# Hybrid mLSTM, stick-breaking and PEER layer: head scores through a per-tile query in place of folded query weights

## The chip, the cores and the metric

One core of a Trainium2 chip runs the whole layer. The metric is the device time of one execution in microseconds; the median of three is given for the kernel before. Engines: PE is TensorE, DVE is VectorE, ACT is ScalarE, POOL is GpSimd, SP is SyncE.

## What is computed

The input has 1024 tokens of width 1024 behind a lead tile that holds 16 meta tokens, so there are nine tiles of 128 tokens. A layer normalises, projects, runs two mixers (an mLSTM with 4 heads and a stick-breaking attention with 8 heads), adds the result to the residual, and then runs a PEER feed-forward: each token has 8 heads, each head picks 16 of 16384 experts. The change touches how a head is scored and one product of the attention:

```python
# peer_ffn, one tile of 128 tokens
q = (xt @ w_query).reshape(T, Hh, 2, PEER_HALF)
s = jnp.einsum('thpc,pnc->thpn', q, sub_keys)
sv, si = lax.top_k(s, K)
...
act = jax.nn.gelu(jnp.einsum('td,thkd->thk', xt, expert_u[eidx]))
return jnp.einsum('thk,thkd->td', g * act, expert_v[eidx])
# stick_breaking_mixer, a block of 128 queries
z = jnp.einsum('bhtd,bhsd->bhts', qb, kh)     # 8 heads of width 64
```

## The kernel before

**Three stages.** In the front PE projects the tiles (a "unit" is one tile and one of six sections of the input weights, written to the tile `xs`) and mixes tile 1. Then comes a stream of slots, numbered from -16. In slot s POOL gathers one row of `expert_u` and one of `expert_v` for each of 128 tokens (512 KB each, an indirect DMA), DVE multiplies the `expert_u` row with the token's row and sums it (L2021, "dot"), and every fourth slot PE adds four `expert_v` rows into `acc` (`sum_set`). Sixteen slots are a head, 128 a tile. Rows wait in rings of slots: four for U and six for V at first, more later (`U_RINGS`, `V_RINGS`). Six tiles go through the stream (`PASSES`); tiles 4 and 6 are "dense": from slot 564 (`DENSE_AT`) on all 16384 experts are computed for them in 128 blocks over 200 slots, on PE (`dense_z`, `dense_out`), while the last gathers run beside it.

**What sets the order.** Every engine has one program, written out slot by slot, and runs it strictly in its order with semaphore waits. The loops at the end of `scalar`, `vector` and `tensor` blocks say what an engine does in a slot. Mixing tile M (2 to 8) is spread over slots from `MIX_AT[M]` on (36, 112, 176, 240, 304, 368, 434); `mixed_at(s)` gives the piece of a slot. Key block i of tile M is one attention step: `z` on PE, three ACT operations for each half of the heads (`ln_z`), DVE `make_sp`, `s` on PE, `exp_a` on ACT, `av` on PE. `hg` is the half: heads of even and odd number, which lie in partitions 0 to 63 and 64 to 127, and whose results go to two different PSUM banks. There are 44 such steps, each with eight `z` products.

**Scoring.** 64 heads are scored (8 tiles of 8 heads, `ROUTED`), head R in slot `SCORES_AT[R]`: heads 0 to 2 in the front's list `ITEMS`, heads 3 to 7 in slots 20, 36, 52, 68 and 84, heads 8 to 55 in slots 109 to 490, heads 56 to 63 in slots 564 to 618. Before any of that the query weights are folded with the keys: 32 folds, each four products of `w_queryT` with `subT` into a PSUM bank and one ACT copy of the bank back over the weights (`fold`). 12 folds stand in `ITEMS`, 12 in slots -6 to 11, 8 in slots 53 to 70 (`FOLD_SLOTS`); the first 24 go to `acc`, the rest to the banks of the units. `scores(R)` is then eight products of `n2T` with the folded weights into bank 7. DVE takes the best 16 of each half of the keys (`best_halves`, L1901, four slots after `scores`) and the picks that follow, in seven pieces in slots +4 to +10. Bank 7 is shared with `turn_idx` and `turn_weights`; each use first waits for all readers of it (`bank7_free`).

Within a slot PE does: `sum_set`, `turn_idx`, `turn_weights`, `scores`, a quarter of a unit (`project`), a fold, the mixing piece, then dense work.

## Time and profile before

| | before |
|---|---|
| median of 3 runs | 3098.28 us (3096.65 to 3100.13) |
| profiled execution, its own time | 3102.96 us |
| its span, first to last instruction | 3101.4 us |
| PE busy | 2620.7 us (85%) |
| DVE busy | 2137.8 us (69%) |
| POOL busy | 1621.3 us (52%) |
| ACT busy | 802.4 us (26%) |
| moved by DMA | 1071.75 MB, mean 346 GB/s |
| mean granted TensorE clock | 0.905 |

An f32 matmul of the program stands in the trace as two matmul records, so eight products are x16. A mean duration of a matmul contains the pipeline's latency; how many microseconds a row of matmuls takes from PE is read from the start of one group to the start of the next, or from the chain of waits. Clock 1.00 is 2.4 GHz, and 0.50 is 1.2 GHz.

### The profile page before, as it was taken

How to read it: one execution, taken by the hardware profiler on the slowest of the kernel's cores; microseconds unless marked ns; L12 is line 12 of the kernel's file. 1: busy time of each engine (PE TensorE's matmuls, PEld its weight loads, DVE VectorE, ACT ScalarE, POOL GpSimd, SP SyncE). 2: the span in 40 equal slices, each digit the busy share in tenths (PEclk: the TensorE clock that was granted, in tenths of full speed). 3: DMA queues.
4: the chain of work that ended last, by engine and by line, in shares of the span. 5: the costliest groups of instructions: out<-in, count | busy, mean ns of one | idle time of the engine just before them, and what ended most of it. 6: DMA issues, size and time to landing. Idle time of an engine off the chain costs nothing.

```text
span 3101.4 us, 36389 instructions
## 1 busy us (share of the span) xinstructions
PE 2620.7 (85%) x12372; PEld 1662.7 (54%) x12372; DVE 2137.8 (69%) x5237; ACT 802.4 (26%) x1766; POOL 1621.3 (52%) x1567
## 2 busy tenths in 40 slices
PE   8999998866877767778687787667999999999998
PEld 6898744323444344444354443445666666666664
DVE  5451646457989879887988887774677755565556
ACT  2231213212323223232243243783111101000001
POOL 0000356577666666655656567665445554455544
PEclk9999999977887878988798798778999999999999
DMA  7103689799999999998989999999999999999998
GB/s 260 49 29 140 229 317 345 282 409 364 382 408 370 397 379 381 385 360 322 403 336 386 353 376 388 393 361 403 371 372 378 383 402 402 403 401 401 402 399 303
DMA packets 338896, 1071.75 MB, mean 346 GB/s; under 512 B 33876, under 2 KB 74136, under 8 KB 337688
## 3 DMA queue, kind: packets, MB, share of 16 engines
q0 software_dynamic: 221184, 805.40, 67.3%
q1 hardware_dynamic: 117528, 264.01, 22.8%
q8 instruction: 100, 1.64, 0.2%
q14 instruction: 84, 0.69, 0.1%
HBM read 1029.03 MB, written 40.26 MB: 345 GB/s over the span
## 4 chain that ended last, share of the span: by engine, by line
PE 55%; DVE 17%; DMA 12%; issue 5%; POOL 5%; ACT 4%; SPq 1%; DVEq 0%; ACTq 0%; POOLq 0%
PE bank L2209 20%; PE xs L2209 15%; PE xs_ahead L2209 14%; DVE work L2021 6%; PE acc L2209 6%; DMA weights<-u_blocks 4%; DMA work<-expert_u,chosen 4%; POOL work L1276 3%; POOL work L1256 3%; DMA work<-expert_v,idx_v 2%; DVE work L1673 2%; DVE work L1681 2%; ACT work L1296 1%; DVE rest L1905 1%; DMA out<-y 1%
## 5 line engine op out<-in xcount | busy, mean ns | idle before, releaser
L1256 POOL DMA_INDIRECT work<-expert_u,chosen x716 | 771.9, 1078 | 837.1 <-DVE dots L2021 351.8
L1276 POOL DMA_INDIRECT work<-expert_v,idx_v x516 | 518.6, 1005 | 399.8 <-PE acc L2209 260.3
L2021 DVE CUSTOM_DVE_ANT_0 work<-work,xs 128x1024 f32<-128x1024 f32 x418 | 506.4, 1216 | 62.4 <-DMA work<-expert_u,chosen 51.4
L2209 PE MATMUL xs_ahead<-work 64*128 64x128 f32 (+3 forms) x1746 | 426.1, 402 | 91.1 <-ACT weights L1296 41.2
L2209 PE MATMUL bank<-weights 128*128 128x256 f32 x2016 | 465.8, 385 | 22.8 <-DMA weights<-u_blocks 22.8
L2021 DVE CUSTOM_DVE_ANT_0 work<-work 128x1024 f32<-128x1024 f32 x298 | 364.1, 1223 | 162.2 <-DMA work<-expert_u,chosen 159.1
L2209 PEld LDWEIGHTS bank<-weights 128*128 128x128 f32 x2016 | 388.6, 193 | 130.6 <-issue 54.4
L2209 PE MATMUL acc<-work,lw 128*32 128x512 f32 x2064 | 338.7, 716 | 91.7 <-DMA work<-expert_v,idx_v 89.4
L2209 PEld LDWEIGHTS xs_ahead<-work 128*128 128x128 f32 (+1 forms) x1746 | 261.9, 214 | 245.2 <-issue 199.4
L1673 DVE TENSOR_TENSOR work<-work,weights 128x256 f32<-128x256 f32 x128 | 54.5, 426 | 371.3 <-ACT work L1544 294.7
L2209 PE MATMUL bank<-weights,n2T 128*128 128x256 f32 x1024 | 265.5, 418 | 23.6 <-ACT lw L1296 22.1
L1544 ACT ACTIVATE work<-bank 128x256 f32<-128x256 f32 x128 | 49.2, 384 | 856.5 <-PE bank L2209 856.5
L2209 PEld LDWEIGHTS bank<-weights,n2T 128*128 128x128 f32 x1024 | 215.0, 214 | 83.9 <-issue 51.0
L2209 PE MATMUL xs<-work 128*128 128x512 f32 x512 | 240.6, 592 | 0.0
L2209 PEld LDWEIGHTS acc<-work,lw 128*32 128x32 f32 x2064 | 67.8, 123 | 251.0 <-issue 150.9
L2209 PE MATMUL xs_ahead<-work,neg_tri 128*128 128x512 f32 (+1 forms) x176 | 115.6, 743 | 86.4 <-DVE work L1681 66.0
L2209 PE MATMUL xs<-work,weights 128*128 128x128 f32 x1472 | 173.9, 280 | 3.4 <-DMA weights<-w_in 3.4
L2209 PEld LDWEIGHTS xs<-work,weights 128*128 128x128 f32 x1472 | 170.6, 196 | 6.0 <-DMA weights<-w_in 3.7
L2209 PE MATMUL xs<-weights,work 128*128 128x512 f32 x368 | 170.7, 608 | 0.0
L1673 DVE TENSOR_TENSOR work<-work 128x512 f32<-128x512 f32 (+3 forms) x156 | 127.9, 822 | 61.9 <-PE xs_ahead L2209 43.6
L1276 POOL DMA_INDIRECT work<-expert_v,chosen x112 | 113.2, 1010 | 55.2 <-issue 33.5
L2209 PEld LDWEIGHTS xs<-work 128*128 128x128 f32 x512 | 97.3, 190 | 68.7 <-issue 62.2
(281 smaller groups left out, 3516.2 us busy)
## 6 DMA issues: line engine op xcount, KB each, us to landing
work<-expert_v SPq DMA_DIRECT2D x128, 512.0 KB, 13.7
weights<-u_blocks SPq DMA_DIRECT2D x126, 512.0 KB, 14.6
work<-kv_dram SPq DMA_DIRECT2D x72, 256.0 KB, 6.2
weights<-w_dram SPq DMA_DIRECT2D x32, 512.0 KB, 20.2
w_dram<-weights SPq DMA_DIRECT2D x7, 2048.0 KB, 11.0
weights<-w_in SPq DMA_DIRECT2D x6, 2048.0 KB, 19.3
work<-expert_u,chosen POOLq DMA_INDIRECT x716, 8.6
mix_dram<-work SPq DMA_DIRECT2D x34, 256.0 KB, 3.3
```

Source lines behind the costliest of these rows:

```text
L1256: pool.indirect_dma_start(out=slot(s), out_offset=None, in_=expert_u, in_offset=bass.IndirectOffsetOnAxis(ap=chosen[:, G % PICKED_HEADS, k ...
L1276: pool.indirect_dma_start(out=slot(s), out_offset=None, in_=expert_v, in_offset=bass.IndirectOffsetOnAxis(ap=picks, axis=0)).then_inc(v_la ...
L1296: return nc.scalar.activation(out_, in_, ACT.Copy, scale=scale)
L1544: nc.scalar.activation(g_d[j % D_G], bank[6][:, 0:D_TOKENS], ACT.Gelu).then_inc(gelu_d_ready, 1)
L1673: return nc.vector.tensor_tensor(out_, a, b, op)
L1681: return nc.vector.scalar_tensor_tensor(out=out_, in0=a, scalar=s, in1=b, op0=op0, op1=op1)
L1905: last = nc.vector.match_replace(spare, values[:, 0:8], src, LOWEST)
L2021: nc.vector.tensor_tensor_reduce(slot(s), slot(s), rows, 1.0, 0.0, ALU.mult, ALU.add, dots[:, d:d + 1]).then_inc(dotted, 1)
L2209: return nc.tensor.matmul(out_, lhsT, rhs, start=start, stop=stop, skip_group_check=True)
```

## The change

The folds are gone. For head R, `query(R)` forms the head's query of this tile, transposed: 2 x 8 products of 128 columns, from the unfolded weights and `n2T`, into bank 7. ACT copies it to a new tile `q_T` (`copy_query`), as the first of the scoring-related work of its next slot, and `scores(R)` is two products of 128 columns of `q_T` with `subT`. In PE's slot the query stands where the scores stood, ahead of the mixing piece; the scores come one slot later (`SCORED_AT = 1`), behind the mixing piece of that slot. The weights are loaded from `w_query` in place of its transpose: the same four loads of 2 MB, in rows of 2 KB where there were rows of 4 KB.

The eight `z` products alternate between the halves of the partitions, where four of the one half came before four of the other.

Smaller parts: the tile `before` is dropped and its two uses are made from `neg_tri` (one product more, once); `gate_inv` becomes `gate_sum` in place; ACT's `square_y` and `rs_y` stand ahead in their slots, and write their unused squares over `q_T`, not `subT`.

```diff
-ACC_FOLDS = 24
+SCORED_AT = 1
...
-put(58.3, ("fold", (0, 4)))
+put(58.3, ("query", 0))
 put(59.5, ("scores", 0))
-put(61.5, ("fold", (4, 8)))
+put(62.2, ("query", 1))
 put(62.5, ("soft", 0))
 put(63.5, ("scores", 1))
 put(65.4, ("picks", 0))
-put(65.5, ("fold", (8, 12)))
+put(65.5, ("query", 2))
 put(66.5, ("scores", 2))
...
-                sp.dma_start(w_qT[i], w_queryT.rearrange("(j c) k -> c j k", c=P)[:, i * Q_EACH:(i + 1) * Q_EACH, :]).then_inc(
+                n = Q_EACH * P
+                sp.dma_start(w_q[i], w_query.rearrange("(k p) n -> p k n", p=P)[:, :, i * n:(i + 1) * n]).then_inc(
...
+            def copy_query(G):
+
+                act.wait_ge(query_done, G + 1)
+                wait(act, scores_done, G)
+                copy(q_T[:, :, :], bank[7][:, 0:2 * P].rearrange("p (j t) -> p j t", j=2)).then_inc(query_copied, 1)
...
                     if s % SLOTS == 0 and 2 <= s // SLOTS + 1 < GT:
                         move_rows(s // SLOTS + 1)
-                    if s - 1 in FOLD_SLOTS:
-                        fold(FOLD_SLOTS[s - 1], FOLD_SLOTS[s - 1] + 1)
+                    for f in finishing(T, n - 1):
+                        square_y(f)
+                    for f in finishing(T, n - 3):
+                        rs_y(f)
+                    for R in [R for R in routed_at(s, SCORED_AT) if R > 2]:
+                        copy_query(R)
...
-                for hg in range(2):
-                    r = slice(SD * hg, SD * hg + SD)
-                    for cc in range(SHP):
-
+                for cc in range(SHP):
+                    for hg in range(2):
+                        r = slice(SD * hg, SD * hg + SD)
                         last = mm(bank[4 + hg][0:m, cc * P:(cc + 1) * P], keys_of(T, i)[r, cc, :], qsT[r, cc, :], cc == 0,
                                   False)
-                    last.then_inc(z_done, 1)
+                        if cc == SHP - 1:
+                            last.then_inc(z_done, 1)
...
+            def query(G):
...
+                bank7_free()
+                seven["queries"] += 1
+                for j in range(2):
+                    n = (2 * h % Q_EACH + j) * P
+                    for k in range(KC):
+                        last = mm(bank[7][:, j * P:(j + 1) * P], w_q[2 * h // Q_EACH][:, k, n:n + P], n2T[:, k, :],
+                                  k == 0, k == KC - 1)
+                last.then_inc(query_done, 1)
+
             def scores(G):
...
-                for k in range(KC):
-                    last = mm(bank[7][:, 0:2 * NKEY].rearrange("p (j n) -> p j n", j=2), n2T[:, k, :],
-                              w_score[2 * h // Q_EACH][:, 2 * h % Q_EACH:2 * h % Q_EACH + 2, k, :], k == 0, k == KC - 1)
+                for j in range(2):
+                    last = mm(bank[7][:, j * NKEY:(j + 1) * NKEY], q_T[:, j, :], subT[:, j, :])
                 last.then_inc(scores_done, 1)
...
                     for R in [R for R in routed_at(at, 0) if R > 2]:
-                        scores(R)
+                        query(R)
                     for part in range(UNIT_PARTS):
                         if at - part in UNIT_SLOTS:
                             project(UNIT_SLOTS[at - part], part, UNIT_PARTS)
-                    if at in FOLD_SLOTS:
-                        fold(FOLD_SLOTS[at], FOLD_SLOTS[at] + 1)
                     for M, m in mixed_at(at):
                         mixing(M, m)
+                    for R in [R for R in routed_at(at, SCORED_AT) if R > 2]:
+                        scores(R)
```

PE's program at the end of the front, from the last transposes of tile 1 (`xs_ahead<-ident,n2T`) to the second head's scores. `acc<-subT,weights` is a fold, `bank<-weights,n2T` the scores as they were, `xs<-...` the units. Before:

```order
L2459 MATMUL xs_ahead<-ident,n2T 128x128 x8
L2209 MATMUL xs<-work,weights 128x128 x16
L2209 MATMUL acc<-subT,weights 128x128 x16
L2209 MATMUL xs<-work,weights 128x128 x16
L2209 MATMUL bank<-weights,n2T 128x256 x8
L2209 MATMUL xs<-y,weights 128x128 x32
L2209 MATMUL acc<-subT,weights 128x128 x16
L2209 MATMUL xs<-weights,work 128x512 x8
L2209 MATMUL bank<-weights,n2T 128x256 x8
```

And with the change, where `bank<-n2T,weights` is the query and `bank<-subT,q_T` the scores:

```order
L2433 MATMUL xs_ahead<-ident,n2T 128x128 x8
L2209 MATMUL xs<-work,weights 128x128 x16
L2209 MATMUL bank<-n2T,weights 128x128 x16
L2209 MATMUL xs<-work,weights 128x128 x16
L2209 MATMUL bank<-subT,q_T 128x128 x2
L2209 MATMUL xs<-y,weights 128x128 x32
L2209 MATMUL xs<-weights,work 128x512 x4
L2209 MATMUL bank<-n2T,weights 128x128 x16
L2209 MATMUL xs<-weights,work 128x512 x4
L2209 MATMUL bank<-subT,q_T 128x128 x2
```

The units stand as they did; the folds between them are gone, and each head has two entries where it had one.

PE's program from slot -6 to the first `sum_set` (`acc<-work,lw`, slot 20), before:

```order
L2209 MATMUL acc<-subT,weights 128x128 x24
L2209 MATMUL xs<-weights,work 128x512 x2
L2209 MATMUL acc<-subT,weights 128x128 x4
L2209 MATMUL xs<-weights,work 128x512 x2
L2209 MATMUL acc<-subT,weights 128x128 x4
L2209 MATMUL xs<-weights,work 128x512 x4
...
L2542 MATMUL bank<-ident,w_spread 128x128
L2209 MATMUL xs<-weights,work 128x512 x4
L2209 MATMUL acc<-work,lw 32x512 x8
L2209 MATMUL bank<-weights,n2T 128x256 x8
L2209 MATMUL xs<-weights,work 128x512 x8
```

With the change:

```order
L2209 MATMUL bank<-subT,q_T 128x128 x2
L2209 MATMUL xs<-weights,work 128x512 x14
L2209 MATMUL bank<-which_eight,c_spread 128x16
L2209 MATMUL xs<-weights,work 128x512 x14
...
L2532 MATMUL bank<-ident,w_spread 128x128
L2209 MATMUL xs<-weights,work 128x512 x4
L2209 MATMUL acc<-work,lw 32x512 x8
L2209 MATMUL bank<-n2T,weights 128x128 x16
L2209 MATMUL xs<-weights,work 128x512 x4
L2209 MATMUL bank<-subT,q_T 128x128 x2
L2209 MATMUL xs<-weights,work 128x512 x4
```

Nothing but unit work is left between the third head's scores and the first `sum_set`, and the scores of head 3 come a quarter of a unit after its query.

ACT's program at two middle heads (tile 3), with the change. `q_T<-bank` is the copy of a query, `work<-xs_ahead`, `work<-work` and `work<-work,one` are one half's `ln_z`:

```order
L1292 ACTIVATE q_T<-bank 128x256
L1454 ACTIVATE work<-xs_ahead 128x512
L1455 ACTIVATE work<-work 128x512
L1456 ACTIVATE work<-work,one 128x512
L1454 ACTIVATE work<-xs_ahead 128x512
L1455 ACTIVATE work<-work 128x512
L1456 ACTIVATE work<-work,one 128x512
```

There was no copy ahead of `ln_z` before: the copy is a new entry in ACT's program for each of the 64 heads, in place of the 32 copies of folds.

## Rows read from the trace of the kernel before

**Rows 1.** Windows: length, busy (count) PE PEld DVE ACT POOL, clock, DMA share, GB/s.

```profile
0.00:340.00 340.00, 325.70 (x2358) 280.99 (x2359) 137.74 (x467) 93.48 (x222) 9.17 (x36) 0.98 0.34 122
340.00:440.00 100.00, 96.47 (x383) 51.51 (x382) 63.45 (x179) 25.70 (x47) 48.63 (x50) 0.98 0.85 293
440.00:612.00 172.00, 146.58 (x653) 72.06 (x652) 100.00 (x257) 45.62 (x94) 102.33 (x93) 0.94 0.86 316
612.00:770.00 158.00, 95.42 (x430) 47.87 (x428) 97.81 (x264) 27.42 (x72) 111.82 (x103) 0.76 1.00 382
770.00:1140.00 370.00, 276.16 (x1384) 154.05 (x1380) 327.43 (x953) 108.38 (x247) 247.57 (x260) 0.83 1.00 392
1540.00:1930.00 390.00, 306.89 (x1574) 174.73 (x1573) 331.21 (x912) 133.64 (x266) 242.81 (x252) 0.87 0.96 367
2135.00:2500.00 365.00, 356.15 (x1296) 239.07 (x1296) 245.10 (x555) 42.88 (x85) 177.43 (x150) 0.99 1.00 380
2500.00:3101.00 601.00, 572.90 (x1995) 373.18 (x1994) 349.30 (x487) 46.01 (x119) 300.30 (x259) 0.98 1.00 389
```

**Rows 2.** Chain of waits, end of the front to slot 32: start us, us, what.

```profile
308.68 3.69 PE acc L2209 x32
312.37 3.57 PE xs L2209 x32
315.94 3.46 PE bank L2209 x16
...
412.18 1.90 PE acc L2209 x16
...
429.16 7.02 DMA work<-expert_v,idx_v
```

**Rows 3.** Timeline of POOL: its gathers, and what ended its idle time.

```profile
328.47 1.15 POOL L1256 DMA_INDIRECT work<-expert_u,chosen  x1 [322.80 <-DVE chosen L1681]
394.59 1.62 POOL L1276 DMA_INDIRECT work<-expert_v,idx_v  x1 [5.72 <-PE xs L2209]
401.96 0.94 POOL L1276 DMA_INDIRECT work<-expert_v,idx_v  x1 [4.50 <-PE acc L2209]
```

**Rows 4.** Groups, shapes apart (two of PE, one of ACT): busy us, mean ns, idle before.

```profile
L2209 PE MATMUL acc<-subT,weights 128*128 128x128 f32 x192 | 23.9, 277 | 0.8 <-ACT weights L1296 0.8
L2209 PE MATMUL xs<-subT,weights 128*128 128x128 f32 x64 | 8.6, 278 | 1.6 <-ACT work L1296 0.8 <-ACT work L1353 0.8
L1544 ACT ACTIVATE work<-bank 128x256 f32<-128x256 f32 x128 | 49.2, 384 | 856.5 <-PE bank L2209 856.5
```

**Rows 5.** Timeline of PE near slot 76: a `sum_set` that waited.

```profile
592.23 3.64 PE L2209 MATMUL acc<-work,lw 128*32 128x512 f32 x16 [7.56 <-DMA work<-expert_v,idx_v]
```

**Rows 6.** Timeline of PE: one whole `z`, then its middle alone.

```profile
1209.67 1.71 PE L2209 MATMUL xs_ahead<-work 64*128 64x128 f32 x16
1210.11 0.72 PE L2209 MATMUL xs_ahead<-work 64*128 64x128 f32 x8
```

**Rows 7.** Chain of waits from 770 to 1930 us, shares by line.

```profile
by line: PE xs_ahead L2209 15.1%; DVE work L2021 14.1%; PE bank L2209 12.2%; issue 8.5%; DMA work<-expert_u,chosen 8.3%; PE acc L2209 6.1%; DVE work L1681 3.8%; POOL work L1276 3.6%; POOL work L1256 3.2%; DVE work L1673 2.5%; DVE rest L1905
```

**Rows 8.** Timeline: the scores of heads 13, 36 and 46, and DVE's first read.

```profile
824.94 3.66 PE L2209 MATMUL bank<-weights,n2T 128*128 128x256 f32 x16
831.56 0.49 DVE L1901 MAX8 srt<-bank 128x8 f32<-128x128 f32 x2
...
1399.20 6.69 PE L2209 MATMUL bank<-weights,n2T 128*128 128x256 f32 x16 [3.77 <-ACT lw L1296]
1405.93 0.50 DVE L1901 MAX8 srt<-bank 128x8 f32<-128x128 f32 x2
...
1649.72 6.02 PE L2209 MATMUL bank<-weights,n2T 128*128 128x256 f32 x16 [3.58 <-ACT lw L1296]
1659.00 0.48 DVE L1901 MAX8 srt<-bank 128x8 f32<-128x128 f32 x2
```

**Rows 9.** Waits of PE from 2200 to 3060 us: total, times, longest.

```profile
PE bank L2209 <- DMA weights<-u_blocks: 14.5, 5, 3.5
```

More of the change, by code:

```diff
@@ L610, in program @@
         neg_s = sb("neg_s", [P, P], BF16)
-        before = sb("before", [P, P])
         neg_tri = sb("neg_tri", [P, P])
@@ L1198, in select @@
                                    pattern=[[-sign, P]], channel_multiplier=sign).then_inc(fills, 1)
-            for tile, value in ((ident, 1.0), (ident_h, 1.0), (neg_m, 0.0), (neg_s, 0.0), (before, 1.0),
+            for tile, value in ((ident, 1.0), (ident_h, 1.0), (neg_m, 0.0), (neg_s, 0.0),
                                 (neg_tri, -1.0), (ones, 1.0), (tri, 1.0), (valid, 1.0),
@@ L1212, in _ @@
             select(neg_s, -1, ALU.is_gt, NEG)
-            select(before, -1, ALU.is_gt, 0.0)
             select(neg_tri, 1, ALU.is_ge, 0.0)
@@ L1625, in _ @@
                     copy_rows(1)
-                if kind == "fold":
-                    fold(*what)
+                if kind == "query":
+                    copy_query(what)
                 if kind == "soft":
@@ L1661, in _ @@
                         gelu_d(j)
-                    for f in finishing(T, n - 1):
-                        square_y(f)
-                    for f in finishing(T, n - 3):
-                        rs_y(f)
                     for M, m in mixed_at(s):
@@ L1861, in make_sp @@
                 v = sp_[hg].rearrange("p (c t) -> p c t", c=SHP)
-                TT(v, v, before[:, :].unsqueeze(1).broadcast_to([P, SHP, P]), ALU.mult).then_inc(sp_ready, 1)
+                STT(v, neg_tri[:, :].unsqueeze(1).broadcast_to([P, SHP, P]), 1.0, v, ALU.add, ALU.mult).then_inc(sp_ready, 1)
             def add_later(T, i, hg):
@@ L1996, in weigh @@
                 dve.wait_ge(soft_ready, R + 1)
-                STT(w16[:, G % 2, :], dots[:, a:a + TOPK], gate_inv[:, R:R + 1], gate[:, G % PICKED_HEADS, :],
+                STT(w16[:, G % 2, :], dots[:, a:a + TOPK], gate_sum[:, R:R + 1], gate[:, G % PICKED_HEADS, :],
                     ALU.mult, ALU.mult).then_inc(w16_ready, 1)
@@ L2258, in bank_free @@
                 if before:
-                    kind, what = before
-                    if kind == "unit":
-                        pe.wait_ge(unit_taken, ORDINAL[what])
-                    else:
-                        pe.wait_ge(fold_copied, what + 1)
+                    pe.wait_ge(unit_taken, ORDINAL[before[1]])
             def project(u, part, parts=2):
@@ L2466, in turn_picks @@
                 pe.wait_ge(n2T_copied, LAST)
-                mm(bank[6][:, 0:P], ones[:, :], before[:, :])
+                mm(bank[6][:, 0:P], ones[:, :], neg_tri[:, :], True, False)
+                mm(bank[6][:, 0:P], ones[:, :], ones[:, :], False, True)
                 for a in range(len(DENSE)):
@@ L2506, in dense_out @@
                 last.then_inc(out_d_done, 1)
-            seven = {"scores": 0, "picks": 0, "weights": 0}
+            seven = {"queries": 0, "scores": 0, "picks": 0, "weights": 0}
             def bank7_free():
+                wait(pe, query_copied, seven["queries"])
                 wait(pe, scores_free, seven["scores"])
@@ L2618, in _ @@
                         mixing(1, m)
-                if kind == "fold":
-                    fold(*what)
+                if kind == "query":
+                    query(what)
                 if kind == "scores":
```

80 lines of the change are left out of this document (30 added, 50 removed).

## Prediction

> **What bounds the kernel now.** I read the stages first, because one mean over the span would hide that the bound changes [rows 1]. In the front PE is busy 325.7 of 340 us; from 340 to 440 it still is 96.5 of 100, while the DMA share is 0.85. From 440 to 612 PE has 146.6 of 172 and the DMA share is 0.86. From 612 on the DMA share is 0.96 to 1.00 at 367 to 392 GB/s, DVE is busy 85 to 88% of the middle windows and PE about 75 to 79%: there no engine has the bound to itself. In the dense stage PE is busy 356 of 365 us and 573 of 601, with the DMA share at 1.00.
>
> Then I read the chain [rows 2]. Up to 412 us it is PE alone, folds and old scores among it. Behind that it becomes a loop: a `sum_set` ends, POOL gathers the next `expert_v` rows, and they land 7 us later (429.16 + 7.02), with PE waiting for them. POOL's waits say the same from its side [rows 3]: the first gather waits for the first head's picks, then two gathers wait 5.72 us for a unit and 4.50 us for a `sum_set` that PE was late with. The reader is to see that PE's lateness is paid only up to where this loop takes over. In the middle the chain is a third PE (15.1 + 12.2 + 6.1%), and the rest DVE, DMA and POOL [rows 7]. Last I read how much DVE's first look at the scores lags behind them [rows 8], and what PE still waits for in the dense stage: 14.5 us in five waits for `u_blocks` [rows 9].
>
> **The price of a head.** Old scores are x16 matmul records in 3.46 us [rows 2]. The query is x32 records of 128 columns, which is the form and count of half a unit: 3.57 us. The scores are 4 such records, 4 x 3.57 / 32 = 0.45. A head costs PE 3.57 + 0.45 - 3.46 = +0.56 us; 64 heads, +36 us. The folds took 23.9 + 8.6 = 32.5 us [rows 4]. So PE's total hardly changes; where the work lies changes. The page TensorE: Matmul & The Clock Gate of the Trainium skill (Back-to-back issue gap) speaks against cutting matmuls to 128 columns: a stream of weight load and matmul runs at about 81 ns there where the columns alone need 56. By that ratio, as an estimate, a query would take 3.46 x 81 / 56 = 5.0 us and the 64 of them would cost 90 us more on PE. The trace disagrees: 3.57 against 3.46. I go by the row.
>
> **The price of `z`.** A whole `z` is x16 records in 1.71 us, and eight of them in its middle take 0.72 [rows 6]. At the unit's pace (0.112 us apart, last one 0.27 long) eight would take 7 x 0.112 + 0.27 = 1.05. So at the change of halves three pairs already run side by side. With the halves alternating all eight pairs should: 5 more pairs, 5 x 0.112 = -0.56 us each time, -25 us over 44 steps. This is PE time only: ACT begins with the first half, whose last product comes no sooner, and works on it before it needs the second.
>
> **Front, to slot 32.** Removed: 24 folds, 23.9 us. Added: four heads, 2.2. Two `z`: -1.1. PE would reach its first `sum_set` about 22 us earlier. What can use it? The first picks come earlier by one group of folds less 0.56: 3.69 - 0.56 = 3.1, plus 1.1 from `z`: 4 us is safe. The two waits of POOL, 5.72 + 4.50 = 10.2 us, vanish if PE is early. Together 14; but with only four U and six V slots the loop of gather, 7 us and `sum_set` runs from then on and has its own pace, so I take **-13**. Ends: -4 (the loop takes all but the first gather) and -22 (all of PE's lead counts).
>
> **Slots 32 to 76.** Eight folds, -8.6; three `z`, -1.7; three heads, +1.7. PE is busy 85% here, and the next `sum_set` waits 7.56 us for rows [rows 5], so PE's lead partly runs into that wait. I take half: **-4** (0 to -9).
>
> **Middle, heads 8 to 55.** PE: 48 x 0.56 = +27, 39 `z` = -22, net +5, of which a third is on the chain: +2. ACT gets one copy a head, about 0.4 us by a read of the same size [rows 4], 19 us in 1160; it is a third busy, so I price it at nothing by itself. But PE's scores now stand behind a mixing piece and wait for that copy, and ACT may still be in `ln_z`. So the scores end 1 to 4.5 us later than they did: copy and products 1 us, a mixing piece up to 3.5. Behind them in PE's order wait only the next slot's pieces; DVE reads the scores four slots after the query. Two gathers a slot, 260 in 370 us, make a slot 2.85 us, so the usual head has time; of the 48 I count eight with less than 4 us (first and last 3.0 and 3.3, the least 0.0 [rows 8]). I take +2 for these. Sum **+4** (-5 to +17).
>
> **Dense stage, heads 56 to 63.** PE is full, so 8 x 0.56 = +4.5 goes to the end, unless the later waits for `u_blocks`, 14.5 us, take it in [rows 9]. **+4** (0 to 7).
>
> The rest goes together at nothing: DVE's `STT` for `TT` is the same size, the inversion in place too; the extra product for `neg_tri` is one of 128 columns; the four loads of 2 MB have rows of 2 KB like the input weights' loads, and the first two lie in the front, where the DMA share is 0.34; `square_y` and `rs_y` ahead of the slot's other ACT work are six pairs, of which one falls in the dense stage and could hold a `gelu_d` by a microsecond or two.
>
> Sum: -13 - 4 + 4 + 4 = **-9 us**. The profiled execution took 3102.96 us (span 3101.4), 4.7 us over the median of the runs; its own time becomes 3094, the median 3089.
>
> **Rivals.**
> *All of PE's lead counts.* -22 - 9 and the rest as above: -23, 3075. For it: PE's 96% busy at 340 to 440. Against: the loop after 412. Chance 0.10.
> *The gather loop swallows it.* -4 + 0 + 4 + 4 = +4, or +1 with z's help; 3098 to 3102, no change. For it: rows land 7 us after issue whatever PE does. Chance 0.18.
> *The scores come too late for DVE* (slower). Place: slot +4 of a middle head, `best_halves`, with all dots of DVE behind it. Price: the eight tight heads fall short of 4 us by about 17 us in sum, since one had 0.0 and the last 3.3; DVE is busy 88%, so this is not regained. -9 - 2 + 17 = +6, 3104. It decides once the scores end more than some 3 us later than before. For it: rows 8. Against: most heads have twice that. Chance 0.12.
> *The clock gives it back* (same or slower). Where PE is busy 60% (612 to 770) the granted clock is 0.76, where 75%, 0.83, where 96%, 0.98 [rows 1]. The change thins PE's work in 440 to 612 and spreads it in the middle. If the middle's clock fell by 0.05, its PE time of some 890 us (276 in 370 us, 307 in 390, over the 1160) would grow by 55, a third on the chain: +18, so +9 in all, 3107. The Trainium skill's page TensorE: Matmul & The Clock Gate (Part 1: The HAM clock gate) has the mechanism: throttled is the default, and activity releases it. The rows agree in direction. Against: the middle's PE work grows by 5 us and doesn't shrink. Chance 0.06.
> *Alternating gives no overlap.* `z` would fall to 16 x 0.112 + 0.16 = 1.95 us, +0.24 against 1.71, +11 us of PE time, a third on the chain, +4, and the gain booked for it gone: 3097, no change. Chance 0.03.
>
> **How the numbers follow.** My forecast, a gain of 6 to 18 us, has 0.51. About 0.2% (6 us) is what can be told from no change. Faster: 0.51 + 0.10 = 0.61. Same: 0.18 + 0.03 = 0.21. Slower: 0.12 + 0.06 = 0.18. The range holds forecast and first two rivals with the ends of their terms, and most of the third: 3073 to 3105.
>
> **What would show it.** Right: the first gather about 4 us earlier; no wait of POOL for PE before 412; the first `sum_set` some 14 us earlier, later ones waiting for `expert_v` rows; a query x32 in 3.6 us; `z` x16 in about 1.15 us; MAX8 of L1901 idle only a few us in all; the dense stage about 4 us longer. Wrong: if the shift at 612 us is under 5 us, or the middle grows by more than 10, or `z` stays at 1.7.

## The result, and the profile after

The changed kernel is slower: 3107.6 us median against 3098.7 for the kernel before on the same chip, 18 runs each, ratio 1.0030 with a 95% interval of 1.0018 to 1.0041. Forecast was -9 us; it is +9. Single runs of the changed kernel lie up to 18 us apart here (of the kernel before, up to 25 in the comparisons below), and the profiled execution below (3101.91 us, span 3100.3) is one of the quicker ones of its kernel. So times are compared by ratios, and traces by how long a stretch takes and by what waits in it.

The stages after, in the windows and columns of [rows 1]:

```profile
0.00:340.00 340.00, 325.17 (x2351) 278.46 (x2352) 141.96 (x483) 89.39 (x216) 10.68 (x36) 0.98 0.35 126
340.00:440.00 100.00, 87.97 (x322) 41.80 (x321) 65.39 (x176) 18.07 (x36) 58.90 (x57) 0.95 0.93 330
440.00:612.00 172.00, 137.61 (x622) 65.11 (x621) 97.78 (x253) 43.21 (x89) 107.05 (x97) 0.91 0.88 326
612.00:770.00 158.00, 101.55 (x559) 55.86 (x557) 110.23 (x300) 33.77 (x83) 110.54 (x100) 0.79 0.99 383
770.00:1140.00 370.00, 271.03 (x1655) 159.48 (x1652) 323.79 (x941) 110.42 (x255) 247.20 (x256) 0.85 0.99 386
1540.00:1930.00 390.00, 299.85 (x1801) 177.49 (x1802) 318.46 (x877) 134.77 (x276) 234.00 (x245) 0.86 0.94 356
```

PE has time in 340 to 612 now, POOL gathers more there, and the clock of the middle is about what it was (0.85 and 0.86 for 0.83 and 0.87). In 1540 to 1930 DVE and POOL do less than before (318 and 234 us for 331 and 243): there the kernel falls behind.

How far ahead it is can be read at each slot, from the start of its dot (L2021) in both traces. In us against before, for two executions of the changed kernel:

| slot | 32 | 64 | 128 | 256 | 384 | 480 | 512 | 544 | 767 |
|---|---|---|---|---|---|---|---|---|---|
| first | -14.3 | -18.1 | -17.3 | -12.9 | -15.2 | -6.9 | -0.8 | -4.5 | -1.0 |
| second | -16.8 | -17.4 | -12.9 | -9.0 | -9.9 | -2.8 | +4.1 | -0.3 | +4.5 |

The front gained what was forecast, and slots 128 to 512 lost it. First gather and first `sum_set`, timelines of POOL and PE (the first gather was at 328.47 [rows 3], the first `sum_set` at 399.73):

```profile
324.35 1.15 POOL L1252 DMA_INDIRECT work<-expert_u,chosen  x1 [319.04 <-DVE chosen L1681]
```

```profile
383.82 1.92 PE L2209 MATMUL acc<-work,lw 128*32 128x512 f32 x16 [1.66 <-DMA work<-expert_v,idx_v]
```

What PE waited for in the middle, 675 to 1930 us: total, times, longest. Before, then after:

```profile
PE xs_ahead L2209 <- DVE work L1681: 66.0, 38, 6.2
PE xs_ahead L2209 <- DVE work L1673: 29.7, 15, 3.0
PE bank L2209 <- ACT lw L1296: 22.1, 10, 5.2
```

```profile
PE xs_ahead L2209 <- DVE work L1681: 87.2, 38, 6.6
PE acc L2209 <- DMA work<-expert_v,idx_v: 55.2, 11, 7.7
PE bank L2209 <- ACT q_T L1292: 47.3, 14, 6.7
PE bank L2209 <- ACT lw L1292: 24.5, 10, 5.8
```

The first two rows of before are to be read together. Part of `make_sp` ended in a `TT` there (L1673) and is an `STT` (L1681) now, so PE's wait for `make_sp` went from 95.7 to 87.2 us and didn't grow. Before had no wait for `q_T`.

And DVE, 770 to 1930 us:

```profile
DVE work L2021 <- DMA work<-expert_u,chosen: 49.3, 43, 2.9
DVE work L1681 <- ACT work L1456: 45.2, 15, 6.3
DVE srt L1901 <- PE bank L2209: 20.6, 8, 4.8
```

Two waits are new: PE's for the copy of the query, and that of DVE's MAX8 for late scores, eight times where before had one of 1.1 us. Which one is paid is what the experiments ask.

**A head that PE waits for.** Head 51, timeline of PE, then of ACT:

```profile
1765.87 3.79 PE L2209 MATMUL bank<-n2T,weights 128*128 128x128 f32 x32
1769.50 1.00 PE L2209 MATMUL bank<-work 128*128 128x64 f32 x8
1770.43 1.16 PE L2209 MATMUL xs_ahead<-work 64*128 64x128 f32 x16
1775.91 1.12 PE L2209 MATMUL bank<-subT,q_T 128*128 128x128 f32 x4 [4.32 <-ACT q_T L1292]
```

```profile
1771.68 0.60 ACT L1454 ACTIVATE work<-xs_ahead 128x512 f32<-128x512 f32 x1 [5.85 <-PE xs_ahead L2209]
...
1774.87 0.72 ACT L1456 ACTIVATE work<-work,one 128x512 f32<-128x512 f32 x1
1775.50 0.36 ACT L1292 ACTIVATE q_T<-bank 128x256 f32<-128x256 f32 x1
```

The query is done at 1769.7. ACT is idle until `z` is done, then runs the six operations of `ln_z` of the query's own slot, and copies the query only behind them, as first work of its next slot. PE, which has nothing between its `z` and the scores, waits 4.3 us for a copy of 0.36 us. Eleven middle heads wait over 1 us for `q_T`, 46 us in sum. The copy itself is short; what is long is the time that it stands behind `ln_z`.

### The profile page after: what moved, and what is told of

Read it like the earlier page. It is cut to its first block, busy times and chain, and to the rows that moved or that the text cites. A ratio compares the mean times of both kernels' runs of the same rounds, so it can differ in the third digit from the quotient of the medians.

```text
span 3100.3 us, 38702 instructions
## 1 busy us (share of the span) xinstructions
PE 2596.8 (84%) x13398; PEld 1674.3 (54%) x13398; DVE 2138.1 (69%) x5237; ACT 804.7 (26%) x1798; POOL 1632.9 (53%) x1565
## 4 chain that ended last, share of the span: by engine, by line
PE 55%; DVE 14%; DMA 13%; issue 6%; ACT 5%; POOL 5%; SPq 1%; DVEq 0%; POOLq 0%; ACTq 0%
PE bank L2209 20%; PE xs_ahead L2209 16%; PE xs L2209 12%; PE acc L2209 6%; DMA weights<-u_blocks 5%; DVE work L2021 5%; DMA work<-expert_u,chosen 4%; DMA work<-expert_v,idx_v 3%; POOL work L1272 2%; POOL work L1252 2%; DVE work L1673 2%; DVE work L1681 2%; ACT work L1292 1%; DVE rest L1905 1%; ACT work L1455 1%
## 5 line engine op out<-in xcount | busy, mean ns | idle before, releaser
L1272 POOL DMA_INDIRECT work<-expert_v,idx_v x516 | 525.3, 1018 | 413.9 <-PE acc L2209 281.3
L2021 DVE CUSTOM_DVE_ANT_0 work<-work,xs 128x1024 f32<-128x1024 f32 x418 | 506.3, 1216 | 60.7 <-DMA work<-expert_u,chosen 49.6
L2021 DVE CUSTOM_DVE_ANT_0 work<-work 128x1024 f32<-128x1024 f32 x298 | 364.1, 1223 | 159.8 <-DMA work<-expert_u,chosen 156.9
L2209 PE MATMUL xs_ahead<-work 64*128 64x128 f32 (+3 forms) x1746 | 396.7, 392 | 72.4 <-ACT weights L1292 40.8
L2209 PEld LDWEIGHTS xs_ahead<-work 128*128 128x128 f32 (+1 forms) x1746 | 232.8, 206 | 222.3 <-issue 187.2
L1673 DVE TENSOR_TENSOR work<-work,weights 128x256 f32<-128x256 f32 x128 | 54.5, 426 | 376.5 <-ACT work L1543 299.7
L2209 PEld LDWEIGHTS bank<-n2T,weights 128*128 128x128 f32 x2048 | 264.5, 211 | 56.8 <-issue 56.0
L2209 PE MATMUL bank<-n2T,weights 128*128 128x128 f32 x2048 | 269.6, 295 | 28.1 <-ACT lw L1292 24.5
L1673 DVE TENSOR_TENSOR work<-work 128x512 f32<-128x512 f32 (+3 forms) x156 | 128.0, 822 | 55.7 <-PE xs_ahead L2209 37.2
L1272 POOL DMA_INDIRECT work<-expert_v,chosen x112 | 114.3, 1021 | 55.3 <-issue 33.2
```

Of the source, the lines that this page charges most:

```text
L1272: pool.indirect_dma_start(out=slot(s), out_offset=None, in_=expert_v, in_offset=bass.IndirectOffsetOnAxis(ap=picks, axis=0)).then_inc(v_la ...
L1673: return nc.vector.tensor_tensor(out_, a, b, op)
L2021: nc.vector.tensor_tensor_reduce(slot(s), slot(s), rows, 1.0, 0.0, ALU.mult, ALU.add, dots[:, d:d + 1]).then_inc(dotted, 1)
L2209: return nc.tensor.matmul(out_, lhsT, rhs, start=start, stop=stop, skip_group_check=True)
```

## Experiments

All but three, named below, compute the whole reference. Gains and losses are ratios to the kernel before on the same chip; 0.001 is 3.1 us. "Fourth-slot heads" are those whose `SCORES_AT` is the fourth slot of sixteen (3 modulo 16): 23 of the 48 middle heads.

| kernel | median us | ratio, 95% interval |
|---|---|---|
| after, again | 3109.4 | 1.0036 (1.0021 to 1.0051) |
| after, `z` in the old order | 3107.6 | 1.0031 (1.0014 to 1.0047) |
| before, alternating `z` | 3101.8 | 1.0012 (0.9998 to 1.0027) |
| before, no folds | 3081.3 | 0.9942 (0.9923 to 0.9960) |
| after, no copy | 3092.7 | 0.9982 (0.9972 to 0.9991) |
| after, no copy, scores at once | 3102.3 | 1.0002 (0.9989 to 1.0015) |
| copy in the query's slot | 3103.6 | 0.9997 (0.9982 to 1.0013) |
| scores a slot later | 3094.7 | 0.9978 (0.9965 to 0.9992) |
| query, copy, scores a slot earlier | 3089.4 | 0.9967 (0.9954 to 0.9980) |
| the same, but scores a slot later, ahead of the mixing | 3089.0 | 0.9964 (0.9951 to 0.9977) |
| the same, but scores a slot later, behind the mixing | 3082.2 | 0.9935 (0.9916 to 0.9954) |
| before, scores earlier | 3102.5 | 1.0006 (0.9994 to 1.0019) |
| earlier in the other heads alone | 3095.5 | 0.9981 (0.9965 to 0.9997) |
| earlier in fourth-slot heads alone | 3086.2 | 0.9965 (0.9951 to 0.9979) |
| DVE's pieces a slot later | 3127.6 | 1.0094 (1.0075 to 1.0114) |
| that and copy in the query's slot | 3127.3 | 1.0085 (1.0065 to 1.0105) |
| fourth-slot heads, query alone earlier | 3088.3 | 0.9964 (0.9948 to 0.9979) |
| fourth-slot heads, scores alone ahead | 3106.1 | 1.0017 (1.0002 to 1.0032) |

### The change taken apart

**After, again.**

> The change as it is, beside the three that follow, on the same chip. The profile after the change shows a lead of 17 us over the kernel before at slot 128 (where I had forecast 17), and none at slot 512. Round-trip theory: the middle gives the lead back because TensorE waits for ScalarE's copy of the query (50.5 us in all) and the scores reach VectorE late. Order theory: the alternating z products are what costs. Chance theory: the middle is as fast as before and single runs only scatter. All three expect about +9 us over before here.

1.0036: the loss is repeated, as all three theories had it.

**After with the old order of `z`,** and **before with the new one:**

```diff
-for hg in range(2):
-    for cc in range(SHP):
+for cc in range(SHP):
+    for hg in range(2):
```

> The change with the z products in their old order (four of one half, then four of the other). Order theory: the time falls to about 3089 us, a gain of 9 against before, since the alternation was the cost. Round-trip theory: TensorE has 25 us more work of which a third is on the chain, so 0 to 8 us slower than the whole change. The z group returns from 1.15 to 1.71 us.

> The kernel before with nothing but the alternating z products. My price for them: 25 us less work for TensorE, a third of it on the chain, so -4 to -8 us against before. Order theory: slower than before by 10 us or more. If it is within 3 us of before, the overlap exists but saves time that nothing waits for.

1.0031 against 1.0036 for after on the same chip, and 1.0012 for before: `z` brings no time that can be told from none in either kernel. The order theory falls, and so does my price of -4 to -8 us. `z` is shorter nonetheless: its 576 records of 64x128 took 69.7 us before and take 42.7 after.

**Before without the folds.** The scores then use unfolded weights, so they aren't the reference's; work and order are those of before less 32 folds.

```diff
-                if kind == "fold":
-                    fold(*what)
...                                   # the slots' folds and the waits on them go too
```

> The kernel before without its 32 folds: the scores multiply with the unfolded weights and so are not the reference's; everything else is as before. It prices the removal by itself. My forecast: -17 us at slot 128, and no loss after it, so -15 to -18 us in the end. If the gain at slot 128 is there but is gone at slot 512, the middle gives back any lead, whatever the scoring costs, and the round-trip theory falls.

0.9942, a gain of 18 us, which at slots 128, 512 and 767 reads -19.1, -19.9 and -18.8 us: nothing is given back on the way. So the folds are worth 18 us, as forecast (-13 and -4 for the front and the slots behind it), and the rest of the change costs 28.

### The round trip, and the late scores

**No copy.** ACT's copy and both waits on it are gone; the score products read `n2T` in place of `q_T`, so the scores aren't the reference's. In a second kernel they also stand directly behind the query.

```diff
...                                   # copy_query does nothing
-                wait(pe, query_copied, seven["queries"])
-                    last = mm(..., q_T[:, j, :], subT[:, j, :])
+                    last = mm(..., n2T[:, j, :], subT[:, j, :])
```

> The kernel after with the ACT copy of the query left out: the two score products read n2T in place of q_T, so the scores are not the reference's; query and score products stay on PE in the same places and number. Against the kernel before without folds (3081 us) the kernel after (3108 to 3109 us) gives back 27 us. Theory A (the round trip through ACT: PE waits 50.5 us for the copies, ACT 201 us for the queries): that goes, 3085 to 3092 us, and PE's wait for q_T is 0. Theory B (the scores end too late for DVE, whose best_halves then starts late): the scores still stand behind a mixing piece, only the copy's part of the lateness goes; 3098 to 3104 us. Theory C (PE's added products, 0.56 us a head, count in full, 36 us): unchanged, 3105 to 3110 us.

> As the kernel without the copy, and for heads 3 to 63 the score products stand directly behind the query, ahead of the mixing piece of the same slot, where the kernel before had its scores. What is left of the change in a head is PE's work alone. Theory A: no more than 2 us faster than the kernel without the copy. Theory B: another 8 to 15 us, to 3085 to 3092 us. Theory C: 3105 to 3110 us still. PE's work by my price, 8 x 0.56 = 4.5 us in the dense stage and a few in the middle on 3081: 3086 to 3092 us under A and B.

Without the round trip 0.9982, 16 us under after: theory A's, 0.7 us over its range. PE's wait for `q_T` is 0, MAX8 still sits idle 34.4 us (of which 12 are head 0), so late scores alone aren't the loss.

The second kernel missed for A and B alike: MAX8's idle fell to 16.2 us and the time rose to 1.0002. It has neither round trip nor late scores, and its products stand where the old scores stood, and yet it is 19 us slower than the kernel before without folds. From slot 104 to 512 its trace takes 1262.0 us for 1238.1, and from slot 544 to the end 1051.6 for 1049.0. So most of these 19 us lie in the middle and are neither of the two waits. Theory C, that PE's added products count in full, had 3105 to 3110 us for it and came within 3 us; but it had the same for the kernel without the copy and missed there by 12. What is left is PE's products or the smaller parts of the change, which no run takes apart.

**Copy in the query's own slot,** and **scores a slot later** still.

```diff
-for R in [R for R in routed_at(s, SCORED_AT) if R > 2]:
+for R in [R for R in routed_at(s, SCORED_AT) if R > 2 and not (R > 7 and R % 8)]:
     copy_query(R)
...
+for R in [R for R in routed_at(s, 0) if R > 7 and R % 8]:   # behind copy_idx_v and take_unit
+    copy_query(R)
```

```diff
-for R in [R for R in routed_at(at, SCORED_AT) if R > 2]:    # behind the mixing piece
+for R in [R for R in routed_at(at, 2) if R > 2]:            # ahead of it
     scores(R)
```

> The kernel after, whole computation; for heads 8 to 63 but the first of each tile, ACT's copy of the query stands in the query's own slot, ahead of ACT's mixing piece, in place of first in the next slot. PE's order is untouched. Theory A (in after about 13 middle heads have their copy held by an ln_z of the query's slot, and PE waits 2.5 to 6.7 us for each, 50 us in all): PE's wait for q_T falls under 12 us, 3092 to 3099 us. Theory B (the scores' place behind the mixing piece makes DVE late): MAX8's idle stays over 25 us, 3102 to 3108 us. Theory D (where PE's block of 3.7 us of query products lies, in a slot that also has z and a mixing piece, is what costs): nothing moves there, 3104 to 3110 us.

> The kernel after, whole computation, with the scores of heads 3 to 63 one slot later, ahead of the mixing piece of slot +2; query and copy stay. PE has a slot more before it needs the copy. Theory A: PE's wait for q_T falls from 50 to under 20 us, 3094 to 3102 us. Theory B: the scores come later, MAX8's idle grows to 35 to 60 us, 3105 to 3115 us. Theory D: 3104 to 3110 us.

0.9997 and 0.9978, 11 and 17 us under after. With the copy in the query's slot PE's wait for `q_T` all but goes, as A had it, but the time, 3103.6 us, stops short of A's range and lies in B's (3102 to 3108 us with MAX8 idle over 25 us; it is 33.2). So this run gives the copy's place 11 us and doesn't decide for A alone. It has a price of its own: ACT now waits for the query in front of its other work, and DVE once waits 6.4 us for ACT. The second, 3094.7 us, is in A's range and out of B's; yet the wait for `q_T` only fell from 47 to 31 us in the middle, more than A allowed, and MAX8's idle didn't grow as B had it (23.4 us in the middle for 20.6).

Groups of the scores and of MAX8 over the whole run, in the kernel with the copy in the query's slot (busy, mean ns, idle before):

```profile
L2211 PE MATMUL bank<-subT,q_T 128*128 128x128 f32 x256 | 43.9, 295 | 6.4 <-ACT q_T L1292 6.4
...
L1903 DVE MAX8 srt<-bank 128x8 f32<-128x128 f32 x128 | 31.4, 286 | 33.2 <-PE bank L2211 33.1
```

The same two of after:

```profile
L2209 PE MATMUL bank<-subT,q_T 128*128 128x128 f32 x256 | 47.6, 313 | 50.5 <-ACT q_T L1292 50.5
...
L1901 DVE MAX8 srt<-bank 128x8 f32<-128x128 f32 x128 | 31.4, 287 | 32.6 <-PE bank L2209 32.6
```

### Query earlier

For heads 8 to 63 but the first of each tile the query moves one slot ahead of `SCORES_AT`, or two in fourth-slot heads, since the turn of the weights stands one slot ahead of these. The copy is first in ACT's slot behind the query. All kernels with an earlier query have one ACT wait more, for ACT's own `square_y`, which writes over `q_T`.

```diff
-for R in [R for R in routed_at(at, 0) if R > 2]:
-    query(R)
+for R in [...]:                       # the other heads, as they were
+    query(R)
+for R in [R for R in routed_at(at, -1) if R > 7 and R % 8 and scores_at(R) % TOPK != 3]:
+    query(R)
+for R in [R for R in routed_at(at, -2) if R > 7 and R % 8 and scores_at(R) % TOPK == 3]:
+    query(R)
```

> The kernel after, whole computation, with query, ACT copy and scores each one slot earlier for heads 8 to 63 but the first of each tile (49 heads; two slots earlier for those whose scores' slot is the fourth of sixteen, since the weights' turn stands between). Their distance to each other is the same. Theory A: PE waits for the copy as before, 45 to 50 us; 3104 to 3109 us. Theory B: DVE finds its scores ready, MAX8's idle falls from 32.6 to under 20 us, 3092 to 3098 us. Theory C: 3105 to 3110 us.

> The kernel after, whole computation; for the same 49 heads the query is one slot earlier (or two), ACT copies it first in the slot behind, and the scores stand another slot later, ahead of the mixing piece, close to where the kernel before had its scores one slot before. PE has a whole slot's mixing piece and the next slot's sum_set between query and scores. Theory A: PE's wait for q_T falls from 50.5 to under 20 us, 3092 to 3098 us; this would be faster than both kernels. Theory B: MAX8's idle falls a little, 3100 to 3106 us. Theory C: 3105 to 3110 us.

10 and 11 us under the kernel before, both faster than any theory said for them. In both, PE waits less for `q_T` than in after (12.3 and 9.3 us for 50.5), and MAX8's idle is 12 us, none of it in the middle. A and B can't be told apart by them. So the scores went back behind the mixing piece, a slot later: in the 27 other heads to where after has them, in fourth-slot heads to one slot ahead of that.

> As the kernel with query, copy and scores a slot earlier (3089 us, 12 us under before in that comparison), but the scores go back to the slot and place that they have in after, behind the mixing piece of slot +1 (0 for those whose slot is the fourth of sixteen). Theory A: PE never waits for the copy, 3088 to 3094 us. Theory B: DVE has its scores as late as in after, MAX8's idle is 25 us or more and half the gain is lost, 3097 to 3104 us. Theory D: the query's place is what counts, 3088 to 3094 us, with MAX8's idle up.

0.9935: 20 us under the kernel before and 30 under after, the fastest of all. MAX8's idle is 13.0 us, where B wanted 25. But in the fourth-slot heads, in which MAX8 waited in after, the scores stand a slot earlier here; they are left to the runs below.

**The old scores earlier,** 27 heads one slot ahead in the kernel before:

> The kernel before, whole computation, folded weights; its scores stand one slot earlier for the 25 or so heads from 8 on that are neither first of a tile nor in the fourth slot of sixteen. Asks whether the earlier slot would have helped by itself. Theories A and B: before has no round trip and MAX8 waits 2 us behind head 0, so no change, 3096 to 3102 us. Theory D: PE's 3.5 us in another slot than z is worth some of the 20 us that the shifted kernel gained, 3090 to 3095 us.

1.0006. The earlier slot is worth nothing where no copy hangs on it (for the heads outside the fourth slot; the fourth-slot scores can't stand there, as bank 7 is shared with the turn of the weights, and that wasn't tried).

**Which heads.**

> The kernel after, whole computation, with query and copy a slot earlier and the scores where after has them, for the 27 heads from 8 on that are neither first of a tile nor in the fourth slot of sixteen. Theory E (in the middle DVE is the bound: its busy time of 1094 us from slot 104 to 512 was the same in all kernels, and every wait of DVE counts in full; after's loss is the 20 us that MAX8 waits for scores, nearly all in heads of the fourth slot): PE's wait for q_T falls under 20 us, MAX8's idle in the middle stays 18 to 23 us, 3099 to 3107 us. Theory D (the place of PE's block): half of the gain of 20 us, 3093 to 3098 us.

> The other 22 heads alone, those in the fourth slot of sixteen: query and scores two slots earlier, copy two slots earlier. Theory E: MAX8's idle in the middle falls from 21 to under 3 us and the time with it, 3086 to 3093 us, though PE still waits some 25 to 35 us for q_T in the others. Theory D: 3093 to 3098 us. Theory A (PE's waits for the copy count): 3096 to 3104 us.

Under after by 16 us for the 27 other heads, which is D's range and not E's, and by 21 for the 22 fourth-slot ones, which is E's and not D's; together 30. (The edit moves the fourth-slot scores by one slot, not two: they come behind the mixing piece of slot 0 where after has them behind that of slot +1.) PE's waits for `q_T` in the middle fall from 47 us to 13 with the first edit and to 35 with the second, those of MAX8 from 21 us to 22 and to under 1. (The windows below give DVE 1059 us of busy time, not the 1094 of theory E.)

**Is it the wait of MAX8?** In the two kernels that follow DVE asks a slot later in fourth-slot heads; PE's order is that of after. `late(R)` stands for `R > 7 and scores_at(R) % TOPK == 3`.

```diff
-for R in routed_at(s, q):
+for R in [R for R in routed_at(s, q) if not late(R)] + [R for R in routed_at(s, q + 1) if late(R)]:
     PIECES[q](R)
```

> The kernel after, whole computation, PE's and ACT's orders untouched; for the 26 heads from 8 on whose scores' slot is the fourth of sixteen DVE's seven pieces (best_halves to choose) stand one slot later. Theory E: the scores are there when DVE asks, MAX8's idle in the middle falls under 6 us, 3087 to 3095 us, with PE's waits for q_T unchanged at 45 to 50 us. Theory A and D: nothing that they speak of is changed, 3104 to 3110 us.

> Both single edits together: ACT's copy in the query's own slot (alone: PE's wait for q_T 3 us in the middle, but no gain beyond 4 us) and DVE's pieces one slot later for heads in the fourth slot of sixteen. Theory E: as DVE's edit alone, or up to 4 us less, 3084 to 3092 us. Theory A: 3092 to 3098 us. Theory D: 3100 us or more.

Theory E fell here, by 33 us, and A and D, which had no change, missed by 18. The wait of MAX8 is gone as planned (15.8 us idle in all), and the kernel is 19 us slower than after. With the copy in the query's slot as well PE's wait for `q_T` is all but gone too, and the time is the same (3127.3 us). What took the place of MAX8's wait, in after and then with DVE's pieces later:

```profile
L1681 DVE SCALAR_TENSOR_TENSOR work<-xs_ahead,work 128x512 f32<-128x512 f32 (+1 forms) x88 | 60.6, 689 | 56.1 <-ACT work L1456 53.5 <-DVE rest L1673 0.3
```

```profile
L1681 DVE SCALAR_TENSOR_TENSOR work<-xs_ahead,work 128x512 f32<-128x512 f32 (+1 forms) x88 | 60.6, 689 | 76.9 <-ACT work L1456 74.5 <-DVE rest L1673 0.3
```

DVE's wait for `ln_z` in `make_sp` grew by 21 us. So removing MAX8's wait frees no time, and later picks cost some by a way that these runs don't show.

**Query or scores?** The last two kernels move one without the other in fourth-slot heads: the query (and its copy) two slots earlier, or the scores ahead of the mixing piece of slot +1.

> The kernel after, whole computation; for the 22 heads in the fourth slot of sixteen query and copy stand two slots earlier, as in the kernel that gained 21 us on after (3086 us), but their scores stay exactly where after has them, behind the mixing piece of slot +1, so that DVE gets them as late as in after. Theory E, narrowed (MAX8's wait for late scores is what carries the loss): MAX8's idle in the middle stays 15 to 23 us and the time 3102 to 3110 us. Theory D, narrowed (PE's 3.7 us of query products between the weights' turn and the next sum_set, in the fourth slot, make everything behind them on PE late, and MAX8's wait is only where that shows): 3084 to 3093 us.

> The kernel after, whole computation, and the counterpart: query and copy stay in their places; only the scores of the 26 heads in the fourth slot of sixteen stand ahead of the mixing piece of slot +1, in place of behind it. Theory E, narrowed: MAX8's idle in the middle falls from 21 to under 6 us, 3088 to 3096 us. Theory D, narrowed: MAX8's idle falls but other waits of DVE take its place (as they did when DVE's pieces were moved), 3101 to 3110 us.

0.9964 and 1.0017: the query's place is worth 22 us, the scores' place about 5, which isn't clear of noise (the intervals of that and of after overlap, and MAX8 still waits 14.7 us in the middle, where E wanted under 6). Both times are narrowed D's. With the scores where after has them MAX8's wait fell by itself, from 20.6 us in eight to this:

```profile
DVE srt L1905 <- PE bank L2213: 7.8, 5, 3.0
```

**What the place is.** Take head 36, a fourth-slot head. PE in after, from `z` on (its old counterpart is the second pair of [rows 8]):

```profile
1379.79 1.16 PE L2209 MATMUL xs_ahead<-work 64*128 64x128 f32 x16
...
1385.26 6.24 PE L2209 MATMUL bank<-n2T,weights 128*128 128x128 f32 x32 [4.31 <-ACT lw L1292]
1391.43 1.93 PE L2209 MATMUL acc<-work,lw 128*32 128x512 f32 x16
1393.28 1.12 PE L2209 MATMUL xs_ahead<-work,neg_tri 128*128 128x512 f32 x2
1394.24 1.02 PE L2209 MATMUL xs_ahead<-work,ones 128*128 128x512 f32 x2
1395.10 0.61 PE L2209 MATMUL bank<-subT,q_T 128*128 128x128 f32 x4
```

And with the query alone moved:

```profile
1366.95 3.73 PE L2213 MATMUL bank<-n2T,weights 128*128 128x128 f32 x32
...
1372.41 1.16 PE L2213 MATMUL xs_ahead<-work 64*128 64x128 f32 x16
1377.79 3.43 PE L2213 MATMUL acc<-work,lw 128*32 128x512 f32 x16 [4.21 <-ACT lw L1292]
```

In a fourth-slot head `query` stands behind `turn_weights`, and `bank7_free` makes it wait for ACT's copy of those weights, which stands behind `ln_z`. So PE idles 4.3 us and only then does the query. The wait is there either way; moved, it delays the `sum_set`, with the query already done. And the granted clock falls in the wait. Windows of after around it (columns of [rows 1]):

```profile
1377.00:1381.00 4.00, 3.91 (x35) 3.06 (x33) 3.90 (x13) 0.60 (x1) 2.87 (x4) 1.00 1.03 405
1381.00:1385.20 4.20, 0.00 (x0) 0.00 (x0) 4.06 (x10) 3.95 (x7) 3.29 (x4) 0.80 0.95 345
1385.20:1388.30 3.10, 3.04 (x14) 3.07 (x15) 3.00 (x9) 0.00 (x0) 0.90 (x1) 0.50 1.03 399
1388.30:1391.50 3.20, 3.20 (x24) 3.08 (x26) 3.20 (x6) 0.00 (x0) 0.00 (x0) 0.68 0.90 367
```

The query behind the wait takes 6.24 us where it otherwise takes 3.73; moved, the slow stretch falls on the `sum_set`, 3.43 for 1.93. Wait, query and `sum_set` are 4.31 + 6.24 + 1.93 = 12.5 us of PE in after, and 3.73 + 4.21 + 3.43 = 11.4 with the query moved. The old scores pay the same in the kernel before: 6.69 us behind a wait of 3.77 [rows 8].

That 1.1 us is no price for the other heads: PE waits for `lw` in ten middle heads, and over 2 us in four of them. What holds for all is the order. Over the 23 fourth-slot heads of the middle, the end of the next `sum_set` lies 8.9 us behind the end of ACT's `lw` copy on average, in before and in after, and 4.9 us with the query moved (19 of the 23 move). The products no longer stand between the weights and the `sum_set` that needs them. How this becomes 22 us of the whole isn't worked out. Since before has the same 8.9 us, these 22 us aren't what the change lost; whether before could gain them too wasn't tried.

**DVE's busy time doesn't change.** From the dot of slot 104 to that of slot 512 the length differs by up to 48 us between kernels, and DVE's busy time (third count) by no more than 2. Before, after, the fastest, and the one with DVE's pieces a slot later:

```profile
693.54:1931.52 1237.98, 937.63 (x4761) 531.73 (x4757) 1059.49 (x3018) 385.15 (x835) 790.08 (x816) 0.84 0.97 374
```

```profile
675.66:1930.73 1255.07, 940.36 (x5723) 562.46 (x5719) 1059.68 (x3019) 401.86 (x883) 796.63 (x817) 0.85 0.96 369
```

```profile
671.02:1902.95 1231.93, 938.16 (x5723) 565.31 (x5719) 1058.02 (x3018) 403.16 (x883) 788.32 (x817) 0.87 0.98 376
```

```profile
675.93:1954.24 1278.31, 955.99 (x5719) 570.78 (x5713) 1059.05 (x3018) 400.83 (x879) 790.55 (x817) 0.84 0.95 363
```

Every change of the middle's length is a change of DVE's idle time; but which row of DVE shows it says little on who made it late.

## Why the prediction was wrong, step by step

- **Bounds.** Right for the front. For the middle I split PE's time by its share of the chain, a third. For `z` the third was worth nothing, and for the added products no run tests it. What the sum lacked were waits of PE: taking out the 47 us in which it waits for `q_T` gave back 16.
- **The price of a head.** Right. A query takes 3.73 to 3.79 us where nothing slows it (3.57 forecast). Over the 48 middle heads it averages 4.32 us in after, and the old scores 4.31 in before. The four score records take 0.61 us as a group of their own (0.45). The rule of 81 for 56 ns per matmul, which the page TensorE: Matmul & The Clock Gate of the Trainium skill (Back-to-back issue gap) has for a back-to-back stream, would have made it 5.0 as an estimate; 3.73 disagrees, for these f32 products of 128 columns. What 128 columns cost is right; what the products cost where they stand is open (the kernel without copy and with scores at once).
- **The price of `z`.** Right in size, 1.16 us for 1.71 (1.15 forecast), wrong in worth: nothing. I wrote that ACT begins with the first half, which comes no sooner; and behind `z` PE then waits for ACT. In head 36 the wait for `lw` became 4.31 us where it was 3.77 [rows 8]: the 0.55 us went into the wait. By the two runs on `z` the -1 to -2 us booked for `z` in the early slots and the -22 of PE time in the middle should have been dropped.
- **Front, to slot 32,** -13: measured -14.3 and -16.8. First gather 4.1 us earlier, first `sum_set` 15.9 earlier (14 forecast). The two waits of POOL for PE before 412 us shrank, but to 1.6, 2.6 and 2.0 us, and didn't vanish. **Slots 32 to 76,** -4: the lead grew by 2 us to slot 72 in the first trace and shrank by 3 in the second.
- **Middle, +4 (-5 to +17).** Here it failed. From slot 104 to 512 the two traces lost 17.1 and 17.4 us, at the upper end of the term. The failed step is that PE's wait for the copy was left out of the sum: "it is a third busy, so I price it at nothing by itself", and "Behind them in PE's order wait only the next slot's pieces". I saw that ACT may still be in `ln_z`, but counted that only as lateness for DVE. A third busy on average, ACT was busy 3.95 of the 4.20 us behind `z` in head 36 (window 1381.00 to 1385.20) and in head 51 it held the copy so long that PE waited 4.3 us for it; such waits come to 46 us in eleven middle heads. What the runs showed in place of nothing is 11 to 17 us: no copy gave back 16, the copy in the query's slot 11, the scores a slot later 17, the query earlier in the other heads 16. The last two take out only a part of the wait (31 and 13 us are left), so the microseconds of waiting are no measure of the gain.
- **Late scores,** +2. The eight tight heads are there, eight waits of MAX8 and 20.6 us, but by the run with the scores alone ahead they are worth about 5 us, not clear of noise. The sign that I named, MAX8 idle only a few us in all, was a bad one: it is idle 17.0 us in the kernel before, nearly all of it ahead of 360 us.
- **Dense stage,** +4: from the dot of slot 544 to that of slot 767, the last, 1027.4 and 1028.8 us for 1023.9, so +3.5 and +4.9. Right.
- **The rivals.** None has it. "The scores come too late for DVE" gave 3104 with chance 0.12 and came nearest in what the profile shows; by the runs its wait carries little of the loss. "The clock gives it back" hit the time, 3107, but not by its mechanism: the granted clock of the middle stayed. What was missing was a rival for PE held by ACT. The sum of "Alternating gives no overlap" is off: without `z`'s gain the terms give about 9 us more, and with the added 4 it comes to 3102, not 3097; the case didn't arise.
- **The range.** The upper ends of the terms are -4, 0, +17 and +7, together +20 or 3118 us; the range stopped at 3105, and the result, 3107.6, lies between the two.

Summed: folds -18, round trip +16, dense +4; that leaves 8 us of the 28 to the rest, of which the scores' place may be some 5. The parts come from separate runs and don't add exactly, as the runs on the two groups of heads show: 16 and 21 us alone, 30 together. Left open: why the kernel with neither round trip nor late scores is 19 us over before without folds, and why its scores directly behind the query cost 6 us against scores behind the mixing piece, without a wait of PE for `q_T` or more of MAX8's to show for them.

## What to carry to other kernels

A step that goes from one in-order engine through another and back makes the first wait for what stands ahead of it in the second engine's queue at that moment, not for its own duration: look up what the second engine does just then, since a mean load doesn't tell. Part of the wait is paid, here a third. Put the first half of such a step a slot earlier, ahead of waits that the engine has anyway, and the second where it was or nearly; here that turned +9 us into -20, more than the loss, since the moved products also got out of the way of a `sum_set`. And try a wait before calling it the cause: MAX8's was removed and the kernel became 19 us slower.

## What was unexpected of the hardware

Idling can cost PE more than the idle time. In head 36 of after the granted clock was 1.00 before a wait of 4.2 us, read 0.50 (1.2 GHz) for the next 3.1 us of full work and 0.68 in the 3.2 us behind that, so that 3.73 us of products took 6.24. Eight f32 products that alternate between halves of the partitions take 1.16 us where four and four take 1.71; at the unit's pace eight pairs side by side would take 1.05.
